# Spreading the sample queries over 128 partitions: by broadcast reads from HBM where TensorE matmuls did it, in a one-layer decoder step

## The reference

```python
def _stick_breaking(q, k, v, q_pos):
    z = jnp.einsum('bqhd,bshd->bhqs', q, k).astype(jnp.float32) * HEAD_DIM ** -0.5
    strict = (jnp.arange(L, dtype=jnp.int32)[None, :] < q_pos[:, None])[None, None]
    log_keep = jnp.where(strict, jax.nn.log_sigmoid(-z), 0.0)
    after = lax.cumsum(log_keep, axis=3, reverse=True) - log_keep
    a = jnp.where(strict, jnp.exp(jax.nn.log_sigmoid(z) + after), 0.0)
    o = jnp.einsum('bhqs,bshd->bqhd', a.astype(v.dtype), v)
```

## Time and profile before

| | us |
|---|---|
| median of 3 runs | 723.5 |
| lowest and highest run | 722.53 and 727.0 |
| profiled execution, its own time | 723.5 |
| its span from first to last instruction | 721.6 |
| granted TensorE clock, mean | 0.925 |
| PE busy, DVE busy | 615.5 (85%), 378.0 (52%) |
| DMA | 228.79 MB, mean 317 GB/s |

### The profile page before, as it was taken

How to read it: one execution, slowest core, us unless ns; L and a number is a source line. 1 busy time by engine, 2 the same in 40 slices (tenths; PEclk the granted TensorE clock), 3 DMA queues, 4 the chain that set the end, 5 groups by cost and what they waited for, 6 DMA issues and landing times.

```text
span 721.6 us, 8341 instructions
## 1 busy us (share of the span) xinstructions
PE 615.5 (85%) x3320; PEld 344.7 (48%) x3320; DVE 378.0 (52%) x668; ACT 154.2 (21%) x292; POOL 112.1 (16%) x100
## 2 busy tenths in 40 slices
PE   3998999999999968997679999188988978979764
PEld 2775774487788844543468546132322313223111
DVE  3087999998679998632003132652442422414024
ACT  2015215512510254544100010011011001010001
POOL 1632613211111452641200000000000000000001
PEclk9999999999899989999859997579999989999896
DMA  9998988849866489899989585109999999999921
GB/s 332 409 417 318 346 334 315 321 161 383 304 233 233 161 312 341 350 427 426 423 255 404 178 348 175 59 4 375 420 419 419 420 421 421 419 421 421 397 102 60
DMA packets 66609, 228.79 MB, mean 317 GB/s; under 512 B 14099, under 2 KB 16675, under 8 KB 56300
## 3 DMA queue, kind: packets, MB, share of 16 engines
q1 hardware_dynamic: 51116, 137.70, 49.1%
q0 software_dynamic: 12672, 88.09, 31.1%
q10 hardware_dynamic: 2784, 2.51, 1.0%
HBM read 223.68 MB, written 4.60 MB: 316 GB/s over the span
## 4 chain that ended last, share of the span: by engine, by line
PE 58%; DMA 13%; DVE 12%; SPq 8%; ACT 5%; issue 3%; ACTq 1%; POOL 0%; DVEq 0%
PE PS L591 14%; PE PS L1122 5%; SPq L442 5%; DMA arena<-in_w_down 5%; DMA arena<-in_cache_v_a,page_idx 5%; PE PS L1104 4%; PE PS L1130 4%; PE PS L1028 4%; PE PS L1044 4%; PE PS L1170 3%; SPq L447 2%; PE PS L954 2%; PE PS L740 2%; PE PS L728 2%; DMA arena<-in_cache_v_b,unit_idx 2%
## 5 line engine op out<-in xcount | busy, mean ns | idle before, releaser
L591 PE MATMUL PS<-xT,arena 128*128 128x264 f32 x608 | 146.4, 401 | 0.6 <-DVE xT L1588 0.3
L591 PEld LDWEIGHTS PS<-xT,arena 128*128 128x128 f32 x608 | 118.5, 197 | 24.4 <-issue 2.0
L1596 DVE TENSOR_TENSOR arena<-arena,x_rows 128x2048 f32<-128x2048 f32 x32 | 73.1, 2283 | 20.0 <-ACT x_rows L1233 19.9
L1600 DVE TENSOR_REDUCE x_rows<-arena 128x32 f32<-128x2048 f32 x32 | 73.2, 2288 | 1.1
L520 POOL DMA_INDIRECT arena<-in_cache_k_b,unit_idx x32 | 39.4, 1231 | 142.2 <-DVE x_rows L1600 137.9
L2043 DVE TENSOR_TENSOR x_rows<-PS,x_rows 128x512 f32<-128x512 f32 (+1 forms) x48 | 33.0, 687 | 46.3 <-PE PS L1130 46.3
L1130 PE MATMUL PS<-temp 128*128 128x512 f32 (+1 forms) x96 | 48.4, 642 | 4.9 <-issue 4.9
L1122 PE MATMUL PS<-arena,temp 128*32 128x512 f32 x384 | 46.0, 613 | 4.3 <-issue 3.2
L1170 PE MATMUL PS<-arena,temp 128*32 128x512 f32 x256 | 34.9, 694 | 16.3 <-DMA arena<-in_w_down 12.5
L520 POOL DMA_INDIRECT arena<-in_cache_v_b,unit_idx x32 | 39.3, 1227 | 52.9 <-PE PS L954 32.6
L581 POOL TENSOR_TENSOR small<-small,consts 128x1 f32<-128x1 f32 x3 | 2.6, 867 | 270.1 <-DVE small L2095 270.1
(11 more groups left out here) (346 smaller groups left out, 870.5 us busy)
## 6 DMA issues: line engine op xcount, KB each, us to landing
arena<-in_w_down SPq DMA_DIRECT2D x32, 1024.0 KB, 17.1
arena<-in_w_gate SPq DMA_DIRECT2D x48, 512.0 KB, 14.0
arena<-in_w_up SPq DMA_DIRECT2D x48, 512.0 KB, 14.3
arena<-in_w_in SPq DMA_DIRECT2D x9, 2048.0 KB, 9.9
temp<-in_w_gate SPq DMA_DIRECT2D x12, 512.0 KB, 14.6
temp<-in_w_up SPq DMA_DIRECT2D x12, 512.0 KB, 14.8
temp<-in_w_out SPq DMA_DIRECT2D x1, 4096.0 KB, 14.5
x_rows<-in_x_prompt SPq DMA_DIRECT2D x2, 1024.0 KB
```

Of the source, the lines that this page charges most:

```text
L591: last = nc.tensor.matmul(PS[0:m, n % 2, 0:T], w[:, k, c0:c0 + m], xT[:, k, :], start=(k == 0), stop=(k == KC - 1))
L1596: nc.vector.tensor_tensor(k_ring[:, u], k_ring[:, u], q_all[:, b % 2:b % 2 + 1, :].to_broadcast([P, 4, H * HD]), ALU.mult).then_inc(s_mul, 1)
L1600: nc.vector.tensor_reduce(z_s[:, b, :].rearrange("p (h r) -> p r h", r=R)[:, 4 * u:4 * u + 4, :], k_ring[:, u].rearrange("p r (h d) -> p r ...
```

## The change

The eight PE matmuls and seven of their eight places in the numbering of PSUM results, the eight ACT copies, `pick_row` and its DVE copy go. `q_row` moves to another place in SBUF. ACT writes it to a new HBM tensor `q_dram` (16 KB) and each query is read back from there by a DMA with a broadcast source, 2 KB to each of 128 partitions (256 KB): for sequences 0 and 1 SP issues it, behind a wait for the write and ahead of the wait and load that stood next in its list; for 2 to 7 ACT issues it (`load_q`) where its copy stood, behind the same wait on `s_mul`. DVE's unit waits for the landing (`s_q`) and no longer for ACT's copy.

```diff
-        q_row = oaT.rearrange("p k t -> p (k t)")[0:NS, 0:H * HD]
-        pick_row = obT.rearrange("p k t -> p (k t)")[0:NS, 0:NS * P]
+        q_row = temp[0:NS, 8192:8704]
+        q_dram = nc.dram_tensor("q_dram", [NS, H * HD], F32).ap()
...
+            sp.wait_ge(s_qdram, 16)
+            for b in range(2):
+                sp.dma_start(q_all[:, b, :], q_dram[b:b + 1, :].to_broadcast([P, H * HD])).then_inc(s_q[b], 16)
             sp.wait_ge(s_proj, N_QI)
             sp.dma_start(w_a[:, :, :], w_in[:, :, O_QA:O_QA + 512]).then_inc(s_wa, 16)
...
-            def spread_q(b):
-                m = M_QB[b]
-                pe.wait_ge(s_trf, max(m - 1, M_Q + 1))
-                nc.tensor.matmul(PS[:, 2 + m % 2, :], pick_row[:, b * P:(b + 1) * P], q_row, start=True, stop=True
-                                 ).then_inc(s_tr, 1)
-            pe.wait_ge(s_pick, 1)
-            spread_q(0)
...
             nc.scalar.activation(q_row, PS[0:NS, 2 + M_Q % 2, :], ACT.Copy, scale=HD ** -0.5).then_inc(s_trf, 1)
-            def spread_q(b):
-                m = M_QB[b]
-                act.wait_ge(s_tr, m + 1)
-                if b >= 2:
-                    act.wait_ge(s_mul, 4 * (b - 1))
-                nc.scalar.copy(q_all[:, b % 2, :], PS[:, 2 + m % 2, :]).then_inc(s_trf, 1)
+            act.wait_ge(s_trf, M_Q + 1)
+            act.dma_start(q_dram, q_row).then_inc(s_qdram, 16)
...
+            act.wait_ge(s_qdram, 16)
+            def load_q(b):
+                act.wait_ge(s_mul, 4 * (b - 1))
+                act.dma_start(q_all[:, b % 2, :], q_dram[b:b + 1, :].to_broadcast([P, H * HD])).then_inc(s_q[b % 2], 16)
...
-            spread_q(2)
+            load_q(2)
...
-            nc.vector.tensor_copy(pick_row.rearrange("p (b n) -> p b n", b=NS),
-                                  ident[0:NS, 0:NS].unsqueeze(2).to_broadcast([NS, NS, P])).then_inc(s_pick, 1)
...
                 if u == 0:
-                    dve.wait_ge(s_trf, M_QB[b] + 1)
+                    dve.wait_ge(s_q[b % 2], 16 * (b // 2 + 1))
```

More of the change, by code:

```diff
@@ L335, in decoder_step @@
         s_v = [sem(f"s_v{u}") for u in range(8)]
-        s_pick, s_mul, s_kused, s_ls, s_sps, s_scan, s_ts, s_as, s_vused, s_owide, s_apad0, s_apad1 = (
-            sem(n) for n in ("s_pick", "s_mul", "s_kused", "s_ls", "s_sps", "s_scan", "s_ts", "s_as", "s_vused",
+        s_q = [sem(f"s_q{i}") for i in range(2)]
+        s_qdram, s_mul, s_kused, s_ls, s_sps, s_scan, s_ts, s_as, s_vused, s_owide, s_apad0, s_apad1 = (
+            sem(n) for n in ("s_qdram", "s_mul", "s_kused", "s_ls", "s_sps", "s_scan", "s_ts", "s_as", "s_vused",
                              "s_owide", "s_apad0", "s_apad1"))
@@ L366, in decoder_step @@
         vb_rows = a["cache_v_b"][0].rearrange("n (q r) h d -> (n q) (r h d)", r=4)
[L369 to L378, removed]
+        M_Q, M_WI = 0, 1
+        M_KIDX = 2
+        M_KA = M_KIDX + 2 * NS
+        M_ROWS = M_KA + 4 * NS
+        M_NEW = M_ROWS + 12
         M_AFT = [M_NEW + 1, 0]
@@ L720, in turn_ka @@
                 for which in range(2):
[L721 to L724, removed]
+                    m = M_KA + 8 * pair + 2 * j + which
                     pe.wait_ge(s_trf, m - 1)
@@ L737, in _ @@
                         turn_ka(pair, j + 1)
-                    pe.wait_ge(s_trf, m_ka(8 * pair + 2 * j + 1) + 1)
+                    m = M_KA + 8 * pair + 2 * j
+                    pe.wait_ge(s_trf, m + 2)
                     for which in range(2):
                         last = nc.tensor.matmul(PS[which * 32:(which + 1) * 32, ACC + j, :], qaPad[:, pair + 4 * which, :],
-                                                kT_s[:, 4 + 2 * j % 4 + which, :], start=False, stop=(pair == 3))
+                                                kT_s[:, 4 + m % 4 + which, :], start=False, stop=(pair == 3))
                     last.then_inc(s_kT2_used, 1)
@@ L771, in _ @@
                     m += 1
-            spread_q(6)
             count_above(13)
@@ L1263, in _ @@
             relu_kidx(3)
-            spread_q(2)
+            load_q(2)
             for c in range(4):
                 evac(N_QA + c, qaT[:, c, :])
-            spread_q(3)
+            load_q(3)
             evac(N_KA, kaT)
@@ L1273, in _ @@
                 if j == 12:
-                    spread_q(4)
-                m = m_ka(j)
+                    load_q(4)
+                m = M_KA + j
                 act.wait_ge(s_tr, m + 1)
@@ L1278, in _ @@
                     act.wait_ge(s_kT2_used, j // 2 - 1)
-                nc.scalar.copy(kT_s[:, 4 + j % 4, :], PS[:, 2 + m % 2, :]).then_inc(s_trf, 1)
+                nc.scalar.copy(kT_s[:, 4 + m % 4, :], PS[:, 2 + m % 2, :]).then_inc(s_trf, 1)
             for j in range(4):
@@ L1284, in _ @@
             act.wait_ge(s_sc, 1)
-            spread_q(5)
+            load_q(5)
             for c in range(8):
@@ L1298, in _ @@
             act.wait_ge(s_trf, m)
-            spread_q(6)
+            load_q(6)
             for names, dst in zip(outs, places):
@@ L1359, in _ @@
                 if c == 4:
-                    spread_q(7)
+                    load_q(7)
                 if c == 7:
```

13 lines of the change are left out of this document (3 added, 10 removed).

## The result

The changed kernel takes 725.84 us (median of 20 runs, 721.18 to 734.06) against 721.9 us for the kernel before (20 runs, 715.8 to 727.69): a ratio of 1.0058, 95% interval 1.0036 to 1.0082. The forecast was a gain of 1.1 us; the measurement is a loss of about 4, within 1% and inside the range given, on the other side of nothing.

A forecast was written before the change was run, and what follows sets the result against it. PE and DVE were taken as tight together up to about 270 us. DVE's lateness of 2.2, less 0.5, 2.1, 0.8 and 1.05, gave -2.2 us; the clock's 1.1 made it -1.1: 723.5 to 722.4 us, range 718.5 to 730.

The forecast's parts named there:

- What bounds the kernel: PE and DVE tight together up to about 270 us; DVE's lateness at 213 us goes to the end.
- L: Moment DVE may start unit 0, after query write and read: 38.78 before, forecast about 46, bounds 43.4 and 57.
- break-even: Time is 676.4 + L while PE waits for DVE at the first count; no change at L = 47.1.
- rival 2: First broadcast late at unit 0: L 48 to 54, chance 0.22; beyond, 0.12. Mild form, several-piece turns: L 49, 725.4 us.
- DVE from L on: Units 0 to 3 take 20.3 us, the 4.41 us wait goes, unit 4 starts at 66.3.
- rival 3: Same L; standstills at 58 and 87 us cost two low clock stretches, 724.1 us, or none, 721.3; chance 0.13.
- The returns: Spreads PE no longer makes, from the third on, give back 1.05, 2.1, 0.8 and 1.05 us up to 213 us.
- D: DVE's lateness at unit 4 and the first count, L - 43.8: forecast 2.2 us.
- The clock: One low stretch behind PE's standstill of about 5 us at the first count: 1.7 us lost, 1.1 net.
- The later queries cost nothing: Queries 2 to 7 by reads: landings in time, ACT's issue costs what its copy did; cost nothing.
- The whole gain: Rival: query comes by 41.3 us, all spreads count, no clock loss; 716.7 us, chance 0.06.
- Off the path: Rival: DVE's 16 us of waits swallow any delay; only start and spreads behind 160 us count; 721.3 us, chance 0.05.

The follow-up runs named there:

- e2: Kernel before, with queries 0 and 1 by DMA write and reads, 2 to 7 still by PE; 1.0073 of before.
- e9: Kernel before, no DMA of a query, unit 0 held until the third qi chunk's evacuation; 1.0080 of before.
- e3: Changed kernel, all transfers kept, but sequence 0 multiplies by constants without waiting for its query; DVE waits at unit 4, ACT between later reads; 0.9949 of before.
- e15: Changed kernel unedited, measured again beside e12 and e13; 0.9998 of before.
- e0: Changed kernel unedited, measured again with a second profile; 1.0038 of before.
- e4: Changed kernel, with 7 extra PE matmuls ahead of the qiPad wait and 4 ahead of the first count; 1.0086 of before.
- e1: Changed kernel, but queries 0 and 1 spread by PE and ACT as before, 2 to 7 by reads; 0.9958 of before.
- e6: e1 with the read of query 2 issued earlier, among the copies of the indexer's turns; 0.9980 of before.
- e13: Changed kernel with the read of query 4 issued three times, eight copies earlier, nobody waiting for the extra two; 1.0020 of before.
- e14: e10 measured again, beside e12 and e13: changed kernel with query 4's read issued eight copies earlier; 1.0054 of before.
- e10: Changed kernel with only the read of query 4 issued eight copies earlier; 1.0004 of before.
- e8: Kernel before, no DMA of a query, unit 0 held until the second qi chunk's evacuation; 1.0024 of before.
- e12: Changed kernel with the read of query 4 issued three times in its late place, nobody waiting for the extra two; 1.0079 of before.

## Why the prediction was wrong

*What bounds the kernel.* Right in the main. The two engines are tight, and a wait put on DVE at 40 us was followed to 213 us; e2 and e9, 5.3 and 5.8 us slower, show that it goes to the end. Not all of it does: the kernel that reaches this step earliest (e3, 205.6 us) has a median of 719.0 us and the latest (e9, 221.3) 728.4, so 15.7 us there are 9.4 in the time. Missing from the picture is ACT, which holds PE at the gate chunks.

*L, the start of unit 0.* The first step that failed, a mis-sized term. Forecast 46, measured 47.6 (46.7 to 48.4 in the seven profiles of this kernel and of those that differ from it only in query 4's reads), which is past the forecast's own break-even of 47.1. The write's leg was forecast at 3.3 us up to SP's issue (36.6 to 39.9) and took 4.6 (36.24 to 40.80). The read's was 6.0 and took 6.8. Both were built on the 4.1 us of `sample_buckets`, and that row is from a stretch with room: from 73 to 78 us before's DMA engines moved 279 GB/s, where from 36 to 42 they moved 415. By the forecast's formula, 676.4 + 47.6 = 724.0 us: half a microsecond slower in place of 1.1 faster. The Trainium skill ("DMA: Bandwidth & Descriptors", section on the anatomy of one DMA) would put the two legs at 4.6 us, an estimate, by a fit made for DMAs that GpSimd issues; the trace has 11.4 for these two, issued by ACT and SP, and the measurement decides. The mild form of rival 2 had L = 49 and 725.4; its time is nearly what came, but its L is not, so that is no sign for its long turns.

*DVE from L on.* Right: 20.3 us were forecast to unit 4 and 67.67 - 47.61 = 20.1 measured; the wait at L1616 went. Wrong in the main line was where PE would stand: 3.6 of its 5.2 us are before the `qiPad` matmuls and only 1.6 at the first count. Only rival 3 had named a standstill at 58 us.

*The returns.* Neither their sum nor their places were right. Forecast were 4.45 us against D; in the first profile 3.6 came back, from 3.6 us late to 0.0 at 212.5. From the first count to the tenth DVE waits for nothing in before and in after (27.9 us from the first to the fifth, then 19.5 and 19.4 to the eighth), so spreads 3 and 4 returned nothing up to there, though the chain of before had both on it (96.81 and 121.20 us): where two engines are tight the chain names only one of them; PE even waited 0.7 us for DVE at the fifth count. Behind the eighth the returns were 1.1, 1.3 and 1.2 us. L1669 is 1.0 us late in e15's profile and 5.6 in e0's.

*The clock.* Expected behind PE's standstill at the first count for one stretch, 1.1 us. In the profiles of after and e15 there was none behind the count (1.00 in 96 to 100 us, row above); in e9 with 5.4 us of standstill there was. In e0 the clock was low there, and DVE's answers up to the fifth count were no later for it. So in that place the term was nothing. The low stretch at 60 us is off the path (e4). But a stretch did cost where the forecast had none, behind PE's 2.3 us standstill for ACT at the gate chunks. The same 16 matmuls in after and in e0:

```profile
199.44 3.83 PE L590 MATMUL PS<-xT,arena 128*128 128x264 f32 x16 [2.28 <-ACT arena L1336]
203.37 5.51 PE L590 MATMUL PS<-xT,arena 128*128 128x264 f32 x16 [2.27 <-ACT arena L1336]
```

That is 1.7 us on the path, at a granted clock of 0.59 from 204 to 208 us, so mostly the lower level of 1.2 GHz; e1, e3, e6, e13 and e14 have the same 5.4 to 5.5 us in this place, and e15 and e10, with the low stretch one chunk earlier, lose nothing by it, since ACT holds PE anyway. It is no mark of the change: e8, the kernel before with a hold on unit 0, has the standstill and the low stretch too.

*"The later queries cost nothing."* Not right as it stands, and how it fails is open. The forecast asked whether each query lands in time for DVE, and they all do. It did not ask what else the change meets. The gather for PE's L711 is asked for only when PE has emptied its place and lands with little to spare: it is two DMAs, and before, the second was issued at 127.10, landed 8.2 us later, and PE needed it at 136.29. Every profile with the later reads has a wait of PE for it, and the four without them (before, e2, e8, e9) have none. In after it landed 8.5 us from its issue, hardly later than before; what moved was the issue, to 130.40, because POOL's issue of the first took 2.44 us where before it took 0.94:

```profile
127.65 2.44 POOL L519 DMA_INDIRECT temp<-in_cache_k_a,page_idx  x1 [1.32 <-PE PS L711]
...
130.40 0.94 POOL L519 DMA_INDIRECT temp<-in_cache_k_a,page_idx  x1 [0.30 <-issue]
```

Those 1.5 us are more than the 0.8 that PE waited, and the wait cost DVE nothing in that profile. In e0 both issues were short (0.93 and 0.94), but the gather took 11.4 us from its issue, with this row.

```profile
141.70 1.09 PE L711 MATMUL PS<-consts,temp 128*128 128x128 f32 x8 [2.11 <-DMA temp<-in_cache_k_a,page_idx]
```

And e0's windows around it, with the low clock that followed:

```profile
140.00:144.00 4.00, 2.06 (x14) 1.83 (x15) 3.89 (x2) 1.09 (x3) 0.00 (x0) 0.91 1.01 426
144.00:148.00 4.00, 4.00 (x20) 1.84 (x20) 0.80 (x5) 1.62 (x3) 0.94 (x1) 0.66 0.89 338
```

PE's busy time is 2.06 of 4 us in the first, and DVE's 0.80 in the second: it waits 3.1 us for PE in this place. That is the 3.2 us which e0 loses against after between the fifth and the eighth count. That the read of query 4 by itself is what does it is not shown, and e14 speaks against it: there this read was issued at 115.7 us and landed 7.0 us later, from 126 to 134 us POOL's queue alone moved data, and still the gather took 10.4 us and PE waited 1.2. What e0, e13 and e14 share is POOL's order of issues: the gathers for the pair ahead of it went out 4 to 6 us later than in before (from 120.3 to 123.4 us against 116.0 and 117.5) and two fetches of unit keys directly behind them, so more may have been queued ahead. Where DVE and PE stand against POOL is thus a rival to the reads' traffic, and no run separates the two.

*The rivals.* The whole gain needed L at 41.3 and did not come; e3, whose DVE starts even earlier, has 0.9949 where the rival had 0.9906. Off the path fell with e3 and e9. The clock behind the two standstills that rival 3 named cost nothing in the profiles of this kernel; behind a third one it cost 1.7 us in e0. Rival 2 in its mild form lies nearest, with an L that came out between it and the forecast.

*Which step failed, and what is open.* Shown is L, 46 forecast and 47.6 measured: 1.6 us, enough to turn the forecast's sign. The rest of the way from -1.1 us to the -0.1, 2.8 and 4.2 of the three measurements is not one term. At L1669 the three profiles are 0.0, 1.0 and 5.6 us late, and e0's 5.6 has two places that the forecast had at nothing: the wait for the gather (3.2 us by the eighth count) and the clock behind the wait for ACT (1.7 us). What sets off the first, the reads' traffic or the new places of DVE and PE against POOL, stays open, as does how often an execution is like e0's and how often like after's.

## What to carry to other kernels

A matmul of 1 us that spreads a row over the partitions is cheap against a write to HBM and a read back, 11.4 us here in a stretch in which the DMA engines are full: leave the first use, which an engine stands waiting for, on the engine, and move only those that have 10 us to spare. A landing time taken from a row is worth what the traffic around that row was. For each added transfer ask two questions, not one: does it land in time, and which transfer with little margin does it, or the engine that it makes late, push. Work taken from an engine returns only where that engine sets the pace; up to the eighth count PE's spreads were free in this kernel, and behind it they counted. And a table of waits cut at a round number of microseconds can hide the longest one just behind the cut.

## What the runs showed of the hardware

An earlier issue moved the landing by only half. In e14's profile the read was issued at 38.8 and unit 0 started at 46.7, in after's 40.8 and 47.6, in e12's 42.4 and 48.4: 3.6 us between the issues, 1.7 between the landings. The Trainium skill says that the DMAs of all issuing engines run on the same 16 engines and interleave ("DMA: Bandwidth & Descriptors", section on issuing engines); the trace fits that, if what is queued on them by then is much the same, which no run here shows.

POOL's issue of an indirect DMA can take three times as long as at other times. Rows of the changed kernel's timeline:

```profile
81.23 2.28 DVE L1572 TENSOR_TENSOR arena<-arena,x_rows 128x2048 f32<-128x2048 f32 x1
81.36 2.97 POOL L519 DMA_INDIRECT temp<-in_cache_k_a,page_idx  x1 [0.30 <-issue]
83.55 2.29 DVE L1576 TENSOR_REDUCE x_rows<-arena 128x32 f32<-128x2048 f32 x1
84.63 0.94 POOL L519 DMA_INDIRECT arena<-in_cache_k_b,unit_idx  x1 [0.30 <-issue]
85.75 2.28 DVE L1572 TENSOR_TENSOR arena<-arena,x_rows 128x2048 f32<-128x2048 f32 x1
86.11 2.74 POOL L519 DMA_INDIRECT arena<-in_cache_k_b,unit_idx  x1 [0.54 <-DVE x_rows L1576]
```

The issues that meet DVE's multiply take 2.7 to 3.0 us and end 0.8 us behind it, the one that begins under the reduction takes 0.94. The 2.44 us at 127.65 above are the same: the multiply there runs from 127.00 to 129.28. So where DVE stands against POOL sets when the keys are asked for; what lies behind it was not tried.

The same kernel has its low stretches of the clock in different places from one execution to the next: between 92 and 96 us e0's windows have 0.57 where after's have 1.00.

```profile
92.00:96.00 4.00, 3.82 (x11) 3.14 (x12) 3.96 (x3) 0.00 (x0) 0.00 (x0) 0.57 1.01 428
```
